# Sample cross-attention: which operand stands and which streams, and one column group per head

## The chip, the cores and the metric

The kernel runs on one core of one Trainium2 chip. The metric is the device time in microseconds; before the change it is the median of three runs.

## The reference, cut to what matters

One layer of a hybrid decoder, for a prompt of 1024 tokens and for a sample group of 8 sequences with 4 tokens each, both with the same weights, d_model 1024, all in fp32. After the mixer comes a cross-attention, 4 heads of 256 dimensions over 256 memory tokens:

```python
def cross_attend(xn, mk, mv, w_xq, w_xo):
    B, L = xn.shape[:2]
    q = (xn @ w_xq).reshape(B, L, N_X_HEADS, X_HEAD_DIM)
    s = jnp.einsum('bqhd,bkhd->bhqk', q, mk.astype(q.dtype)).astype(F32) * (X_HEAD_DIM ** -0.5)
    p = jax.nn.softmax(s, axis=-1).astype(q.dtype)
    o = jnp.einsum('bhqk,bkhd->bqhd', p, mv.astype(q.dtype))
    return o.reshape(B, L, X_WIDTH) @ w_xo
```

For the sample group, keys and values (mk, mv) come from a cache, a separate 1 MB of each for every sequence (8 + 8 MB). An MLP of width 4096 follows.

## The kernel before, in words

Activations stand feature-major in SBUF: hT, and the operand pairs xhi/xlo and yhi/ylo (fp32 split into a high and a low part), each 8 blocks of 128 features by 1056 tokens (1024 of the prompt, 32 of the samples). A weight matrix streams in as "units" of 128 output features: SP loads a unit into raw, ACT makes whi (`split_hi`), DVE makes wlo (`split_lo`, L342), each double-buffered, and TensorE's `product` (L353 to L355) multiplies the unit by a chunk of 352 tokens in 3 x 8 matmuls. There are three chunks. DVE takes the result from PSUM.

The change is in the stage after the prompt's cross-attention. The order of work is written out by hand on every engine, as a list with semaphore waits. On TensorE:

- **Keys**, for each sequence b of 8: `sx_turn(b)` transposes 256 x 1024 keys in 16 transposes (L1035, tile kx; the prompt's probabilities, tile xp, are turned by the same line) into four PSUM banks; then one `xo_product` (unit U_XO + b/2, chunk b%2) runs while ACT and DVE (L1789) evacuate the turned keys to kxT; then `sx_scores(b)` (L1362) multiplies: 16 matmuls whose stationary is a 128x128 block of keys and whose moving operand is 4 query columns.
- **Softmax**: the scores stand keys-major, so DVE copies them to sxT (L1796), TensorE turns them (tile sxT), DVE takes maxima (L1798), ACT the exponential, DVE scales. TensorE meanwhile does both chunks of U_XO + 4, turns the probabilities (tile sxp), and ACT copies them to pxT.
- **Values**, for each of four pairs of sequences: `sx_values` (L1374) twice, each 16 matmuls with a 128x128 block of values as stationary and 4 probability columns moving; then, but for the last pair, both chunks of the next unit.
- **Tail**: ACT and DVE (L1814) make yhi and ylo of the 32 sample tokens from PSUM, and TensorE goes on with w_xo a second time (units U_XB to U_XB + 7), now for chunk 2, which holds the sample tokens.

GpSimd issues the loads of keys (two slots of 1 MB, refilled as soon as the keys of two sequences before are turned) and of the values of sequences 0 to 3; ACT issues those of 4 to 7 (into slots freed by the values of 0 to 3). Ahead of that GpSimd stages the prompt's queries (L676, paced by the prompt's score matmuls of L1311) and copies the sample queries to xqs (L685), since the key slots lie on top of xq. Between the loads it sums squares for the next norm (`xo_squares`). SP's weight loads wait for the split of two units before.

DVE's order in this stage, per unit: evacuate the keys of sequence 2i, add the product to hT (L1781), the same for 2i + 1, then the split of the next unit. An fp32 matmul (not fp32r) leaves two MATMUL and two LDWEIGHTS records, a transpose one of each. Elsewhere in the kernel some lines write into column groups, among them L1117 (window attention; 128 rows, one group of 64 columns, repeated), L1182 (retention state of the prompt, 128 rows, two groups of 64 columns in turn) and L1294 (retention state of the samples, 32 rows, the same two groups in turn).

## Time and profile before

| | before |
|---|---|
| median of three runs | 1763.68 us |
| lowest, highest | 1756.89, 1764.25 us |
| span of the profiled execution, first to last instruction | 1753.1 us |
| TensorE matmuls, busy | 1646.7 us, 94% of the span |
| VectorE, ScalarE, GpSimd busy | 648.0, 443.8, 251.8 us |
| mean granted TensorE clock | 0.946 of full speed |
| read from and written to HBM | 101.19 and 14.16 MB |

The profiled execution is shown by its span; no separate device time of that one execution is given, and the median stands 10.6 us above the span. Times in rows are microseconds from the first instruction. TensorE's busy time is split into PE (matmuls) and PEld (weight loads), which overlap. Busy TensorE is not TensorE at its peak: how many columns stream per weight load, and the granted clock, do not show in that share.

### The profile page before, as it was taken

The page shows a single profiled execution, that of the slowest core. Times are in us where ns is not written, and L with a number is a line of the kernel's source. Part 1 is how long each engine was busy: PE and PEld are TensorE (multiplying, and loading weights), DVE is VectorE, ACT ScalarE, POOL GpSimd, SP SyncE. Part 2 cuts the span into 40 slices and gives each one's busy share as a digit, 9 for nine tenths or more (in the row PEclk, how much of TensorE's full clock was granted, in tenths as well). Part 3 has the DMA queues.
Part 4 walks back from the last instruction along what each step waited for, and adds up shares of the span by engine and source line. Part 5 has one row for each costly group of instructions (what it writes and reads, how often), then busy time and mean ns, then how long its engine had stood idle before and what let it go on. Part 6 is the DMA issues. An engine that isn't in the chain of part 4 may idle for free.

```text
span 1753.1 us, 25903 instructions
## 1 busy us (share of the span) xinstructions
PE 1646.7 (94%) x10206; PEld 1583.2 (90%) x10206; DVE 648.0 (37%) x1170; ACT 443.8 (25%) x779; POOL 251.8 (14%) x310
## 2 busy tenths in 40 slices
PE   5879999988789999789999999999999999999998
PEld 5869777778679999679999999999999999999998
DVE  3532455535544432342221653223322333233322
ACT  4530233323311111241100433003310231023212
POOL 2100100032227500111131400000000000000053
PEclk9989899999869999898887999999999999999999
DMA  5741000010322121022332311111111111111112
GB/s 181 204 182 48 13 25 24 13 45 25 95 96 84 37 95 36 13 97 85 120 109 72 96 49 48 49 48 49 37 48 48 49 48 49 44 40 48 48 36 99
DMA packets 152617, 115.37 MB, mean 66 GB/s; under 512 B 12880, under 2 KB 141968, under 8 KB 152272
## 3 DMA queue, kind: packets, MB, share of 16 engines
q1 hardware_dynamic: 140816, 72.49, 14.2%
q0 software_dynamic: 10576, 37.66, 6.1%
q10 hardware_dynamic: 1152, 4.19, 0.7%
q8 instruction: 51, 0.84, 0.2%
q14 instruction: 22, 0.18, 0.0%
HBM read 101.19 MB, written 14.16 MB: 66 GB/s over the span
## 4 chain that ended last, share of the span: by engine, by line
PE 80%; issue 11%; DVE 5%; ACT 2%; POOL 1%; DMA 1%; ACTq 0%; DVEq 0%; SPq 0%; POOLq 0%
PE ps L353 21%; PE ps L354 20%; PE ps L355 20%; PE ps L1035 5%; PE ps L1374 2%; PE ps L1100 2%; PE ps L1311 2%; PE ps L1329 2%; PE ps L1117 2%; PE ps L1362 2%; DVE wlo L342 1%; DVE xlo L1456 1%; ACT whi L326 1%; PE ps L1175 0%; PE ps L1177 0%
## 5 line engine op out<-in xcount | busy, mean ns | idle before, releaser
L353 PE MATMUL ps<-xhi,whi 128*128 128x352 f32 x1392 | 458.6, 329 | 15.9 <-DVE wlo L342 9.0
L354 PE MATMUL ps<-xlo,whi 128*128 128x352 f32 x1392 | 450.7, 324 | 0.0
L355 PE MATMUL ps<-xhi,wlo 128*128 128x352 f32 x1392 | 450.5, 324 | 0.0
L353 PE MATMUL ps<-yhi,whi 128*128 128x352 f32 x1152 | 381.5, 331 | 3.8 <-DVE xq L1476 1.9
L354 PE MATMUL ps<-ylo,whi 128*128 128x352 f32 x1152 | 376.7, 327 | 0.0
L355 PE MATMUL ps<-yhi,wlo 128*128 128x352 f32 x1152 | 375.6, 326 | 0.0
L353 PEld LDWEIGHTS ps<-xhi,whi 128*128 128x128 f32 x1392 | 265.2, 191 | 28.1 <-issue 17.3
L354 PEld LDWEIGHTS ps<-xlo,whi 128*128 128x128 f32 x1392 | 265.8, 191 | 0.1
L355 PEld LDWEIGHTS ps<-xhi,wlo 128*128 128x128 f32 x1392 | 264.7, 190 | 0.0
L326 ACT ACTIVATE whi<-raw 128x1024 fp32r<-128x1024 f32 x126 | 132.9, 1054 | 437.8 <-PE ps L355 403.1
L353 PEld LDWEIGHTS ps<-yhi,whi 128*128 128x128 f32 x1152 | 223.1, 194 | 4.6 <-issue 2.2
L354 PEld LDWEIGHTS ps<-ylo,whi 128*128 128x128 f32 x1152 | 222.9, 193 | 0.1
L355 PEld LDWEIGHTS ps<-yhi,wlo 128*128 128x128 f32 x1152 | 222.1, 193 | 0.0
L342 DVE TENSOR_TENSOR wlo<-raw,whi 128x1024 fp32r<-128x1024 f32 x130 | 167.9, 1291 | 82.2 <-ACT whi L326 72.7
L1481 DVE TENSOR_TENSOR hT<-ps,hT 128x352 f32 (+1 forms) x120 | 62.7, 523 | 280.2 <-PE ps L355 280.2
L1850 DVE SCALAR_TENSOR_TENSOR relu<-ps,rstd 128x352 f32<-128x352 f32 x96 | 50.3, 524 | 180.4 <-PE ps L355 179.2
L979 ACT ACTIVATE hsq<-relu 128x352 f32<-128x352 f32 x96 | 47.9, 499 | 233.2 <-DVE relu L1850 233.2
L524 POOL TENSOR_TENSOR ss<-hT 128x528 f32<-128x528 f32 (+1 forms) x7 | 6.5, 947 | 669.3 <-DVE hT L1481 655.6
L527 POOL TENSOR_TENSOR sq<-hT 128x528 f32<-128x528 f32 (+1 forms) x50 | 62.9, 1257 | 132.0 <-issue 89.7
L529 POOL TENSOR_TENSOR ss<-ss,sq 128x528 f32<-128x528 f32 (+1 forms) x50 | 66.9, 1337 | 3.9
L1842 DVE TENSOR_TENSOR ylo<-hsq,yhi 128x352 f32 (+1 forms) x96 | 50.5, 526 | 31.2 <-DVE relu L1850 15.8
L716 ACT ACTIVATE yhi<-hsq 128x352 f32 (+1 forms) x96 | 47.8, 498 | 9.8
(271 smaller groups left out, 1548.3 us busy)
## 6 DMA issues: line engine op xcount, KB each, us to landing
raw<-in_w_up SPq DMA_DIRECT2D x32, 512.0 KB
raw<-in_w_down SPq DMA_DIRECT2D x32, 512.0 KB
raw<-in_w_xo SPq DMA_DIRECT2D x16, 512.0 KB
kx<-in_cache_mem_k POOLq DMA_DIRECT2D x16, 512.0 KB, 4.4
raw<-in_w_in SPq DMA_DIRECT2D x14, 512.0 KB, 3.9
spill<-hT POOLq DMA_DIRECT2D x8, 528.0 KB, 6.2
hT<-spill POOLq DMA_DIRECT2D x8, 528.0 KB, 5.0
raw<-in_w_xk SPq DMA_DIRECT2D x8, 512.0 KB
```

Source lines behind the costliest of these rows:

```text
L326: act.activation(whi[:, q], raw[:, q], ACT.Copy).then_inc(s_whi, 1)
L342: dve.tensor_tensor(wlo[:, q], raw[:, q], whi[:, q].bitcast(F32), ALU.subtract).then_inc(s_wlo, 1)
L353: pe.matmul(out, whi[:, q, k, :], x1, start=k == 0, stop=False)
L354: pe.matmul(out, whi[:, q, k, :], x2, start=False, stop=False)
L355: mm = pe.matmul(out, wlo[:, q, k, :], x1, start=False, stop=k == KB - 1)
L527: st.did(pool.tensor_tensor(sq[:, 0:b - a], h, h, ALU.mult))
L529: last = pool.tensor_tensor(ss[:, a:b], ss[:, a:b], sq[:, 0:b - a], ALU.add)
L979: act.activation(hsq[:, b, :], relu[:, b, :], ACT.Square).then_inc(s_sqr, 1)
L1035: return pe.transpose(out, in_, ident[0:n, 0:n])
L1481: return dve.tensor_tensor(chunk(hT, u - m0, c), ps[:, (q + c) % 2, 0:CW], chunk(hT, u - m0, c), ALU.add)
L1842: dve.tensor_tensor(chunk(ylo, u - u0 + q, c), hsq[:, (q + c) % 2, :], chunk(yhi, u - u0 + q, c).bitcast(F32), ALU.subtract).then_inc(s_hl ...
L1850: dve.scalar_tensor_tensor(relu[:, (q + c) % 2, :], ps[:, gemm_bank(u + q, q, c) if q == 0 else (q + c) % 2, 0:CW], 0.0, rstd[:, c * CW:(c ...
```

## The change

Keys and values become moving operands. Queries are kept as qm: for each of the 8 feature blocks and each sequence b a stationary of 32 columns, one per sample token, which is zero but for the 4 columns of b; a score matmul streams 256 keys past it and adds into 32 partitions (one column group per head) of PSUM bank 6, over all sequences. Scores so stand token-major (head, token by key). The copy sxT and its turn go. Probabilities are turned and scattered by ACT into pm, masked in the same way; values stream 256 columns (a head) into a column group per head of bank 2. That output is token-major, so it is copied (osb) and turned (two transposes) ahead of yhi and ylo. GpSimd sets qm and pm to zero. Turned keys are double-buffered by sequence (kT). The second chunk of U_XO + 4 moves behind the turn of the probabilities, and the second chunk of U_XO + 7 behind the last values.

```diff
-        kxT, _ = place("kxT", [P, 2, KB, P], at=at_xl + 24576)
-        sxT, _ = place("sxT", [P, 2, P], at=at_xl)
-        sxp, _ = place("sxp", [P, NM], at=at_xl + 1024)
-        pxT, _ = place("pxT", [P, 2, P], at=at_xl + 2048)
-        xqs, _ = place("xqs", [P, KB, TS], at=at_xl + 32768)
+        kT, _ = place("kT", [P, 2, KB, NM], at=at_xl)
+        qm, _ = place("qm", [P, KB * NB * TS], at=at_xl + 16384)
+        pm, _ = place("pm", [P, 2 * XH * NB * TS], at=at_xl + 24576)
         at_t = at_tab + 4 * 2 * P
+        sxp, _ = place("sxp", [P, NM], at=at_t)
+        osb, _ = place("osb", [P, NM], at=at_t + 4 * NM)
...
+        def own_columns(t):
+            return bass.AP(t, 0, [[t.shape[1], P], [NB * TS, t.shape[1] // (NB * TS)], [TS + DT, NB], [1, DT]])
@@ gpsimd @@
-            pool.tensor_copy(xqs[:], xq[:, :, TP:T]).then_inc(S("sx_q_kept"), 1)
+            pool.wait_ge(s_xs, NQ)
+            pool.memset(qm[:], 0.0).then_inc(S("sx_zeroed"), 1)
+            pool.wait_ge(S("sx_zeroed"), 1)
+            pool.tensor_copy(own_columns(qm), xq[:, :, TP:T].rearrange("p k (b t) -> p k b t", t=DT)).then_inc(S("sx_q_kept"), 1)
...
                 sx_load(pool, b, "cache_mem_v", values_at(b), lambda slot: s_kl[slot])
+            pool.wait_ge(s_xo, NQ)
+            pool.memset(pm[:], 0.0).then_inc(S("sx_zeroed"), 1)
             for m in range(2, KB):
                 xo_squares(m)
@@ scalar @@
-                        wait(act, s_ksc, t - 1)
-                        copy(kxT[:, kb, 0:4, :].rearrange("p k t -> p (k t)"), ps[:, 2 + 2 * kb, :]).then_inc(s_kea, 1)
+                        wait(act, s_ksc, 2 * i + r - 1)
+                        copy(kT[:, r, 0:4, kb * P:(kb + 1) * P], ps[:, 2 + 2 * kb, :].rearrange("p (k t) -> p k t", k=4)).then_inc(s_kea, 1)
...
-            act.activation(sxp[:], ps[:, 7, 0:NM], ACT.Exp, scale=1.0 / 16, bias=wneg[:, 0:1], accum_out=wsum[:, 0:1]).then_inc(S("sx_exp"), 1)
+            act.activation(sxp[:], ps[:, 6, 0:NM], ACT.Exp, scale=1.0 / 16, bias=wneg[:, 0:1], accum_out=wsum[:, 0:1]).then_inc(S("sx_exp"), 1)
             act.wait_ge(S("sx_p_turned"), 1)
-            copy(pxT[:].rearrange("p a r -> p (a r)"), ps[:, 6, 0:2 * P]).then_inc(S("sx_pT_ready"), 1)
+            act.wait_ge(S("sx_zeroed"), 2)
+            copy(own_columns(pm), ps[:, 7, 0:2 * P].rearrange("p (r b t) -> p r b t", b=NB, t=DT)).then_inc(S("sx_pT_ready"), 1)
...
             act.wait_ge(s_vx, NB)
-            copy(yhi[:, :, TP:T], ps[:, 2, 0:KB * TS].rearrange("p (k t) -> p k t", k=KB)).then_inc(s_xoh, 1)
+            copy(osb[:], ps[:, 2, 0:NM]).then_inc(S("sx_o_kept"), 1)
+            act.wait_ge(S("sx_o_turned"), 1)
+            copy(yhi[:, :, TP:T].rearrange("p (h d) t -> p d h t", d=2), ps[:, 3, 0:NM].rearrange("p (d h t) -> p d h t", d=2, h=XH)).then_inc(s_xoh, 1)
@@ tensor, sx_scores(b) @@
-                for kb in range(2):
-                    pe.wait_ge(s_kea, 2 * b + kb + 1)
-                    pe.wait_ge(s_ked, 2 * b + kb + 1)
+                pe.wait_ge(s_kea, 2 * b + 2)
+                pe.wait_ge(s_ked, 2 * b + 2)
+                for dd in range(2):
                     for h in range(XH):
-                        o = kb * P + b * 16 + h * DT
-                        for dd in range(2):
-                            mm = pe.matmul(ps[:, 6, o:o + DT], kxT[:, kb, 2 * h + dd, :], xqs[:, 2 * h + dd, b * DT:(b + 1) * DT], start=dd == 0, stop=dd == 1)
-                    mm.then_inc(s_ksc, 1)
+                        k = 2 * h + dd
+                        mm = pe.matmul(ps[h * TS:(h + 1) * TS, 6, 0:NM], qm[:, (k * NB + b) * TS:(k * NB + b + 1) * TS], kT[:, b % 2, k, :],
+                                       start=b == 0 and dd == 0, stop=b == NB - 1 and dd == 1)
+                mm.then_inc(s_ksc, 1)
@@ tensor, sx_values(b) @@
-                for k in range(KB):
-                    for kb in range(2):
-                        mm = pe.matmul(ps[:, 2, k * TS + b * DT:k * TS + (b + 1) * DT], kx[:, values_at(b) + kb, k * P:(k + 1) * P],
-                                       pxT[:, kb, b * 16 + (k // 2) * DT:b * 16 + (k // 2 + 1) * DT], start=kb == 0, stop=kb == 1)
+                for kb in range(2):
+                    for h in range(XH):
+                        r = (kb * XH + h) * NB + b
+                        mm = pe.matmul(ps[h * TS:(h + 1) * TS, 2, 0:NM], pm[:, r * TS:(r + 1) * TS], kx[:, values_at(b) + kb, h * NM:(h + 1) * NM],
+                                       start=b == 0 and kb == 0, stop=b == NB - 1 and kb == 1)
                 mm.then_inc(s_vx, 1)
@@ tensor, after the eight sequences of keys @@
-            pe.wait_ge(S("sx_s_ready"), 1)
-            for kb in range(2):
-                mm = turn(ps[:, 7, kb * P:(kb + 1) * P], sxT[:, kb, :])
-            mm.then_inc(S("sx_s_turned"), 1)
             pe.wait_ge(s_wlo, U_XO + 5)
             xo_product(U_XO + 4, 0)
-            xo_product(U_XO + 4, 1)
             pe.wait_ge(S("sx_probs"), 1)
             for kb in range(2):
-                mm = turn(ps[:, 6, kb * P:(kb + 1) * P], sxp[:, kb * P:(kb + 1) * P])
+                mm = turn(ps[:, 7, kb * P:(kb + 1) * P], sxp[:, kb * P:(kb + 1) * P])
             mm.then_inc(S("sx_p_turned"), 1)
+            xo_product(U_XO + 4, 1)
             pe.wait_ge(S("sx_pT_ready"), 1)
             for i in range(NB // 2):
+                u = U_XO + 5 + min(i, 2)
                 sx_values(2 * i)
                 sx_values(2 * i + 1)
-                if i < NB // 2 - 1:
-                    u = U_XO + 5 + i
+                if i < 3:
                     pe.wait_ge(s_wlo, u + 1)
                     xo_product(u, 0)
+                if i < 2 or i == 3:
                     xo_product(u, 1)
+            pe.wait_ge(S("sx_o_kept"), 1)
+            for dd in range(2):
+                mm = turn(ps[:, 3, dd * P:(dd + 1) * P], osb[:, dd * P:(dd + 1) * P])
+            mm.then_inc(S("sx_o_turned"), 1)
@@ vector @@
-                        wait(dve, s_ksc, t - 1)
-                        dve.tensor_copy(kxT[:, kb, 4:8, :].rearrange("p k t -> p (k t)"), ps[:, 3 + 2 * kb, :]).then_inc(s_ked, 1)
+                        wait(dve, s_ksc, 2 * i + r - 1)
+                        dve.tensor_copy(kT[:, r, 4:8, kb * P:(kb + 1) * P], ps[:, 3 + 2 * kb, :].rearrange("p (k t) -> p k t", k=4)).then_inc(s_ked, 1)
...
-            dve.wait_ge(s_ksc, 2 * NB)
-            dve.tensor_copy(sxT[:].rearrange("p a r -> p (a r)"), ps[:, 6, 0:2 * P]).then_inc(S("sx_s_ready"), 1)
-            dve.wait_ge(S("sx_s_turned"), 1)
-            st.did(dve.tensor_reduce(wmax[:, 0:1], ps[:, 7, 0:NM], AX.X, ALU.max))
+            dve.wait_ge(s_ksc, NB)
+            st.did(dve.tensor_reduce(wmax[:, 0:1], ps[:, 6, 0:NM], AX.X, ALU.max))
...
-            dve.tensor_tensor(ylo[:, :, TP:T], ps[:, 2, 0:KB * TS].rearrange("p (k t) -> p k t", k=KB), yhi[:, :, TP:T].bitcast(F32), ALU.subtract).then_inc(s_xol, 1)
+            dve.tensor_tensor(ylo[:, :, TP:T].rearrange("p (h d) t -> p d h t", d=2), ps[:, 3, 0:NM].rearrange("p (d h t) -> p d h t", d=2, h=XH),
+                              yhi[:, :, TP:T].bitcast(F32).rearrange("p (h d) t -> p d h t", d=2), ALU.subtract).then_inc(s_xol, 1)
```

## Rows read from the trace of the kernel before

**Rows 1.** The page: busy shares, and the chain that ended last by line.

```profile
PE 1646.7 (94%) x10206; PEld 1583.2 (90%) x10206; DVE 648.0 (37%) x1170; ACT 443.8 (25%) x779; POOL 251.8 (14%) x310
...
PE ps L353 21%; PE ps L354 20%; PE ps L355 20%; PE ps L1035 5%; PE ps L1374 2%; PE ps L1100 2%; PE ps L1311 2%; PE ps L1329 2%; PE ps L1117 2%; PE ps L1362 2%; DVE wlo L342 1%; DVE xlo L1456 1%; ACT whi L326 1%; PE ps L1175 0%; PE ps L1177 
```

**Rows 2.** Stretches (from:to, length; PE, PEld, DVE, ACT, POOL busy (x); clock, DMA share, GB/s).

```profile
794.05:883.31 89.26, 89.26 (x576) 89.26 (x576) 20.23 (x28) 13.36 (x20) 19.04 (x28) 0.81 0.33 112
883.31:895.64 12.33, 11.34 (x54) 11.00 (x55) 2.57 (x7) 1.00 (x4) 3.93 (x6) 0.73 0.15 44
895.64:962.60 66.96, 66.03 (x401) 65.94 (x401) 8.86 (x11) 4.98 (x6) 14.64 (x14) 0.76 0.30 95
962.60:969.30 6.70, 6.70 (x25) 6.70 (x26) 1.23 (x1) 0.41 (x1) 0.00 (x0) 0.56 0.28 78
```

**Rows 3.** Sums of eight stretches each: key turns; then w_xo products; then score matmuls.

```profile
sum 24.48, PE 24.48; mean PE 3.06
...
sum 35.59, PE 35.59; mean PE 4.45
...
sum 29.19, PE 29.19; mean PE 3.65
```

**Rows 4.** The value stretch, with busy time of L1374 alone (PE, PEld).

```profile
895.64:961.60 65.96, 36.79 (x256) 36.94 (x256) 0.77 0.30 96
```

**Rows 5.** Clock: scores, turns, product; state matmuls of L1294; one product at full clock.

```profile
801.30:804.63 3.33, 3.33 (x32) 3.33 (x31) 0.52 (x1) 0.00 (x0) 0.00 (x0) 1.00 0.20 80
804.63:808.04 3.41, 3.41 (x18) 3.41 (x18) 0.69 (x1) 0.60 (x1) 0.00 (x0) 0.50 0.02 5
808.04:811.40 3.36, 3.36 (x23) 3.36 (x22) 0.69 (x1) 1.55 (x2) 1.05 (x2) 1.00 0.40 102
513.30:516.70 3.40, 3.40 (x63) 3.40 (x64) 0.74 (x2) 2.64 (x7) 0.45 (x1) 1.00 0.02 5
...
911.51:915.32 3.81, 3.81 (x25) 1.00 0.00 0
```

**Rows 6.** Timeline of TensorE (start, length, line, tile, shape, records); for L1311 also min/median/max ns.

```profile
769.88 1.04 PE L1035 MATMUL ps<-tab,xp 128*128 128x128 f32 x8
...
775.71 3.62 PE L1311 MATMUL ps<-mkT,stx 128*128 128x256 f32 x16
...
L1311 PE MATMUL ps<-mkT,stx x128: 379/379/767, 708.3 to 779.0; 128*128 128x256 f32 x128
...
201.61 1.93 PE L1117 MATMUL ps<-pT,vtok 128*64 128x512 f32 x4
...
374.85 0.66 PE L1182 MATMUL ps<-vrt,krz 128*64 128x128 f32 x8
375.44 0.44 PE L1035 MATMUL ps<-tab,rk 128*128 128x128 f32 x2
...
374.85 0.42 PEld L1182 LDWEIGHTS ps<-vrt,krz 128*64 128x64 f32 x8
...
513.29 3.71 PE L1294 MATMUL ps<-vrs,kzm 32*64 32x128 f32 x64
```

**Rows 7.** Timeline of GpSimd ahead of the stage; a DMA issue row (median landing).

```profile
760.95 1.04 POOL L676 COPY stx<-xq 128x1024 f32 x1 [8.25 <-PE ps L1311]
...
762.63 2.12 POOL L440 DMA_DIRECT2D kx<-in_cache_mem_k  x4 [0.30 <-POOL xqs L685]
...
kx<-in_cache_mem_k POOLq DMA_DIRECT2D x12, 512.0 KB, 4.3
```

**Rows 8.** Timelines of VectorE and ScalarE around the softmax and at the end.

```profile
880.46 1.66 DVE L342 TENSOR_TENSOR wlo<-raw,whi 128x1024 fp32r<-128x1024 f32 x1
...
884.87 0.42 DVE L1798 TENSOR_REDUCE small<-ps 128x1 f32<-128x256 f32 x1 [0.78 <-PE ps L1035]
...
886.31 0.35 DVE L1556 TENSOR_SCALAR sxp<-sxp,small 128x256 f32<-128x256 f32 x1
...
962.10 0.43 DVE L1814 TENSOR_TENSOR ylo<-ps,yhi 128x256 fp32r<-128x256 f32 x1 [7.37 <-ACT yhi L716]
```

## The prediction

> **What bounds the kernel now.** The page first: TensorE is busy for 94% of the span, and the chain of waits is TensorE lines nearly from end to end; two of them, L1374 and L1362 with 2% each, are the lines that the change rewrites [rows 1]. A microsecond taken out of TensorE's own queue there is a microsecond of the span, unless another engine or a transfer is late next. Then the busy time by stretch, from the first turn of the sample keys (794.05 us) to the end of the first U_XB product (969.30): 89.26 + 12.33 + 66.96 + 6.70 = 175.25 us [rows 2]. TensorE works through nearly all of it, at a mean clock of only 0.56 to 0.81; DVE, ACT and POOL are each busy for a third of it at most, and so are the DMA engines.
>
> The key stage has eight rounds: turns 3.06 us, product 4.45, score matmuls 3.65 on average [rows 3]. In the value stage, L1374 takes 36.79 us, 9.2 per pair of sequences [rows 4]; with 1.0 us of tail (961.60 to 962.60), the six products between share 66.96 - 36.79 - 1.0 = 29.2, or 4.9 each. Both lines load a 128-column stationary to stream four columns past it: 256 records in 29.19 us are 0.114 us each, the spacing of the loads, not of the columns.
>
> The clock is the second thing to see. A stretch of scores alone runs at 1.00; the next, which but for its first 0.3 us holds only turns, at 0.50 (1.2 GHz of 2.4); the next at 1.00 again [rows 5]. So the four-column matmuls are what the clock falls after, and the turns, though slow then, are followed by a rise. In this kernel 64 records in 32*64 tiles, over 3.4 us, ran wholly at 1.00 [rows 5].
>
> **What a new matmul costs.** A score matmul now streams 256 key columns past 32 stationary columns, and its output goes to a quarter of the partitions; four heads in turn use four column groups. Per sequence that is 8 matmuls, or 16 records, in place of 32; the same for values. A record of 256 fp32 columns costs (3.62 - 0.38)/15 = 0.216 us in a row of L1311 [rows 6], 0.38 being a single one's length; one of 128 columns half that, 0.108, with a length of 0.38 - 0.108 = 0.27. *Upper bound:* no overlap between groups, 16 * 0.216 = 3.45 us, what the old scores cost. That records of one column group do not overlap is seen at L1117, which repeats one group: four records of 512 columns in 1.93, 0.48 each where 0.43 would be their columns. *Lower bound:* four at a time, 4 * 0.216 = 0.86. Between them stand L1182 and L1294, which alternate two groups: L1182 has 8 records of 128 columns in 0.66 us, where one after another they would last 8 * 0.108 + 0.16 of tail = 1.02; L1294 has 64 in 3.71, (3.71 - 0.27)/63 = 0.055 each [rows 6]. Groups do overlap, with all 128 rows in use too. The rate that I need for four groups, 0.216/4 = 0.054 per record, is the one at which L1294 was issued, so the queue is no obstacle. I take four at a time. Changing tile shape costs something: from L1182's start to the next line's is 0.59 us, against four slots of 0.108; 0.15 for going in and out [rows 6]. I take 0.24: a score group is 1.1 us, a pair of value groups 8 * 0.216 + 0.22 = 1.95.
>
> The Trainium skill speaks against this (TensorE: Matmul & The Clock Gate, "Packing small matmuls — row/col tiling"): weight loads overlap running matmuls only where the row group differs, and here all four groups share their rows. The trace disagrees: L1182's 8 loads are over in 0.42 us while its matmuls run to 0.66 [rows 6]. Were the page right, an estimate from its columns/1.2 GHz is 27 ns a load, 256 loads, 6.8 us more than my sum.
>
> **The stages, one by one.** *Keys.* Turns: eight full-clock transposes take 1.04 us, (1.04 - 0.27)/7 = 0.11 each [rows 6], so 16 are 1.8 us, if the clock no longer falls. A product alone at 1.00 is 3.81 [rows 5]; 3.9 after another shape. A round is 1.8 + 3.9 + 1.1 = 6.8, eight are 54.4. The idle wait ahead of the first turn stays, and with it that turn's slow clock: 3.06 for 1.8, and some 0.2 on its product, +1.5. Total 55.9 against 89.3.
>
> Cover in that stage: per round DVE is busy for 20.23/8 = 2.5 us and ACT for 1.7 [rows 2], which fits into 6.8. The evacuations' destination is now strided, which I price at nothing. They waited for the previous round's scores, now for those two rounds back: no new wait. K loads: 1 MB is issued when a turn ends and needed two rounds later, 13.6 - 1.8 = 11.8 us; a half lands in 4.3 us, two in about 6 [rows 7]. 112 GB/s at a DMA share of 0.33 over 89.3 us [rows 2] become 112 * 89.3/55.9 = 179 GB/s at a share of 0.53: it fits, though this cover is the thinnest.
>
> *GpSimd ahead of it.* The query copy becomes: wait for the last cross scores, done at 775.71 + 3.62 = 779.3 rather than one block earlier; memset of 2048 columns; copy; then the loads queued behind. A 1024-column copy is 1.04 [rows 7], so the memset is 1 to 3 us, copy 0.4 to 1, four K issues 2.12 [rows 7], landing 4.3 to 6: K data at 779.3 + 3 + 1 + 1.1 + 6 = 790.4 at worst, for turns at 794.05. Cost 0. If that cover were gone, each late microsecond is one. The second memset (after the V issues, ahead of the squares) has over 5 us until ACT needs it: 0; the squares have slack.
>
> *Softmax.* Removed: copy sxT, its turn, and that wait. Added: TensorE reaches the product of U_XO+4 earlier than its weights. DVE's split there lasts 1.66 and starts at 880.46, 0.6 to 0.8 after the product's end (the scores, 3.5 to 3.65 us long, end at 883.31) [rows 8]; so it is done at +2.3 us, scores at +1.1: a new wait of 1.2. Then 3.9; the chain from maximum to probabilities, 884.87 to 886.66, fits inside [rows 8]. Turn 0.25, second product 3.85 (covers ACT's scatter into pm). Total 9.2 against 12.33.
>
> *Values.* 4 * 1.95 = 7.8; 6 * 3.87 = 23.2; the split of each next unit, done 2.3 after a product, is late for values of 1.95: 3 waits of 0.35, 1.0. Total 32.0 against 65.96. V loads have 10 us per pair or more.
>
> *Tail.* The last addition to hT and U_XB's split now follow the last product: ylo is done at 0.6 + 1.66 + 0.43 = 2.7 [rows 8]; two turns and ACT's copies run beside. 2.7 against 1.0, 962.60 less 961.60 [rows 2, 4]. The first U_XB product, 6.70 at clock 0.56 [rows 2], becomes 3.9.
>
> *Sum:* 55.9 + 9.2 + 32.0 + 2.7 + 3.9 = 103.7 against 175.25: 71.5 us less. The span 1753.1 becomes 1681.6. The execution profiled has 10.6 us around its span if it equals the median of 1763.68 (runs reach from 1756.89 to 1764.25): **1692 us**. What a measurement can tell from no change is about 0.5%, 9 us.
>
> **Rivals.** *B, two at a time.* An fp32 matmul is two records in one group; if dispatch holds at the second, only neighbours overlap. Nothing shows four at once; L1294 cannot tell. Then 0.108 per record instead of 0.054: 256 * 0.054 = +13.8, less 2 of waits that vanish: 1704. *C, the clock keeps falling.* Turns stay at 3.06 (+8.8 over seven rounds) and products at 4.45 (+4): 1705; if values bring it down too, six products at 4.9 (+6) and U_XB's 6.70 (+2.8): 1714. For it: short waits are new. Against it: rows 5. The Trainium skill (TensorE: Matmul & The Clock Gate, "PE-mode transpose") says that the full rate does not engage for transposes; here a stretch of hardly anything but turns was followed by 1.00 [rows 5]. By that rule: 1705. *D, the groups do not overlap,* so that the change doesn't do what its placing says: 256 * 0.216 = 55 us; stages 55.9 + 8 * 2.6, 8.0, 28.5 + 23.2, 2.7, 3.9 = 143: 1731. Against it: L1182. *E, slower.* No overlap and the half clock: a 32-column tile counts for little, so the clock falls, and a record costs 0.43. 256 * 0.43 = 110 against the 66 that scores and values take now [rows 3, 4], the rest as before less 3 for the turn gone: +41, 1805. It decides from 69/256 = 0.27 us a record.
>
> **How the numbers follow.** Forecast 0.60 (own range 1682 to 1700), B 0.12, C 0.12, D 0.09, E 0.03, and 0.04 for a late load or memset, half of it costing all the gain. The range 1682 to 1716 takes in the forecast, B and C. Faster 0.95, same 0.02, slower 0.03.
>
> **What would show it.** Right: 16 score records within 1.1 to 1.3 us, starts in fours; turns of 1.8; clock 1.00 from 800 us to the end; a wait of 1.2 for wlo ahead of U_XO+4. B: groups near 2.0. C: digits under 9 in the clock row of the page where turns follow. D: groups of 3.5. The sum is wrong if turns wait on a DMA landing, or if the last key loads start after 785 us.

## The result, and the profile after

The kernel after the change takes 1683.48 us (median of four, 1683.02 to 1685.04) against 1763.23 for the kernel before (four, 1756.89 to 1764.25): a ratio of 0.958, 95% interval 0.955 to 0.961. The forecast was 1692, the range 1682 to 1716.

Its page (busy shares; granted clock in forty slices):

```profile
span 1681.9 us, 25382 instructions
...
PE 1573.4 (94%) x9950; PEld 1498.7 (89%) x9950; DVE 646.8 (38%) x1169; ACT 444.4 (26%) x780; POOL 259.1 (15%) x312
...
PEclk9979899999969999999999999999999999999999
...
PE ps L353 21%; PE ps L354 21%; PE ps L355 21%; PE ps L1047 4%; PE ps L1112 2%; PE ps L1323 2%; PE ps L1341 2%; PE ps L1129 2%; DMA raw<-in_w_xv 1%; DVE wlo L342 1%; DVE xlo L1470 1%; ACT whi L326 1%; DMA raw<-in_w_xk 1%; PE ps L1187 0%; PE
```

The clock row of the page before:

```profile
PEclk9989899999869999898887999999999999999999
```

TensorE's share is 94%, as in [rows 1], so it says nothing of what changed. The two lines with 2% each have left the chain, and 256 of its 10206 matmul records are gone. The digits 8 8 8 7 of the slices where keys and values were are 9 now; the 6 that stands further left in both rows is in the mixer (482 to 526 us before, where TensorE is busy for 37.3 of 43.8 us at a mean clock of 0.67), which the change does not touch.

The stretches after, in the order of [rows 2]: keys, softmax, values, tail, first U_XB product, and all five together.

```profile
794.50:850.05 55.55, 55.55 (x448) 49.12 (x448) 19.04 (x28) 13.36 (x20) 16.86 (x25) 0.97 0.55 183
850.05:859.40 9.35, 8.17 (x55) 7.87 (x51) 2.81 (x6) 1.90 (x4) 7.78 (x9) 1.00 0.21 58
859.40:890.67 31.27, 31.27 (x275) 26.82 (x274) 6.56 (x10) 3.56 (x4) 13.04 (x12) 1.00 0.54 186
890.67:892.70 2.03, 0.17 (x3) 0.00 (x1) 2.03 (x4) 1.33 (x2) 1.45 (x1) 1.00 0.00 0
892.70:898.30 5.60, 5.60 (x25) 5.60 (x26) 1.32 (x1) 0.00 (x0) 2.04 (x2) 0.70 0.64 186
794.50:898.30 103.80, 100.76 (x797) 89.41 (x798) 31.76 (x46) 20.15 (x30) 41.16 (x47) 0.97 0.51 169
```

Keys 55.55, softmax 9.35, values 31.27, tail 2.03, U_XB product 5.60, together 103.80, where [rows 2] sum to 175.25. In the clock column, keys, softmax and values have 0.97 to 1.00 in place of 0.73 to 0.81; the U_XB product has 0.70. TensorE's timeline in the first two rounds, which answers to [rows 3] and [rows 6] (start, length, line, tile, shape, records):

```profile
794.50 3.34 PE L1047 MATMUL ps<-tab,kx 128*128 128x128 f32 x16 [2.63 <-issue]
...
801.86 1.07 PE L1373 MATMUL ps<-kT,qm 128*32 128x256 f32 x16
802.86 1.97 PE L1047 MATMUL ps<-tab,kx 128*128 128x128 f32 x16
804.58 0.41 PE L353 MATMUL ps<-yhi,whi 128*128 128x352 f32 x1
...
808.57 1.07 PE L1373 MATMUL ps<-kT,qm 128*32 128x256 f32 x16
...
859.40 1.93 PE L1387 MATMUL ps<-kx,pm 128*32 128x256 f32 x32
...
890.46 0.38 PE L1047 MATMUL ps<-tab,osb 128*128 128x128 f32 x2
892.70 0.43 PE L353 MATMUL ps<-yhi,whi 128*128 128x352 f32 x1 [1.86 <-DVE ylo L1826]
```

A score group is 1.07 us and a pair of value groups 1.93. Read one by one, the records start in fours, 7 ns apart, and one four follows another after 0.215 us, the spacing at which records of 256 columns follow each other elsewhere (0.216 in the row of L1311 [rows 6]): all four groups stream at the same time. The turn at 802.86 runs at full clock, 1.72 us to the product's first record; the one at 794.50, behind 2.63 us of idle, is still slow. A round is 808.57 - 801.86 = 6.71 us.

TensorE's waits in the same stretch (total, times, longest):

```profile
PE ps L1047 <- issue: 2.6, 1, 2.6
PE ps L353 <- DVE ylo L1826: 1.9, 1, 1.9
PE ps L353 <- DVE wlo L342: 1.2, 1, 1.2
```

The first was there before. The third is the new wait of 1.2 that the prediction had named, the second the tail's. From the first turn to the first MLP matmul the stage took 203.64 us before and takes 132.55 now, 71.1 less; the span fell by 71.2, from 1753.1 to 1681.9. Outside the stage next to nothing moved: the first turn starts at 794.50 for 794.05, and what follows the stage lasts 754.9 us for 755.4. The whole stage before, as a window:

```profile
794.05:997.69 203.64, 200.25 (x1220) 199.57 (x1221) 57.44 (x69) 35.26 (x44) 56.11 (x59) 0.81 0.32 102
```

Cut into stretches of 2 us, that mean clock is 78.5 us at half clock (a granted clock of 0.50). The stage after has 6.8 us of it, behind the idle at 794.50 and behind the tail.

### The profile page after: what moved, and what is told of

Same layout as the page of the kernel before. It is cut to its first block, busy times and chain, and to the rows that moved or that the text cites. A ratio compares the mean times of both kernels' runs of the same rounds, so it can differ in the third digit from the quotient of the medians.

```text
span 1681.9 us, 25382 instructions
## 1 busy us (share of the span) xinstructions
PE 1573.4 (94%) x9950; PEld 1498.7 (89%) x9950; DVE 646.8 (38%) x1169; ACT 444.4 (26%) x780; POOL 259.1 (15%) x312
## 4 chain that ended last, share of the span: by engine, by line
PE 78%; issue 11%; DVE 5%; DMA 2%; ACT 2%; POOL 1%; DVEq 0%; SPq 0%; ACTq 0%; POOLq 0%
PE ps L353 21%; PE ps L354 21%; PE ps L355 21%; PE ps L1047 4%; PE ps L1112 2%; PE ps L1323 2%; PE ps L1341 2%; PE ps L1129 2%; DMA raw<-in_w_xv 1%; DVE wlo L342 1%; DVE xlo L1470 1%; ACT whi L326 1%; DMA raw<-in_w_xk 1%; PE ps L1187 0%; PE ps L1189 0%
## 5 line engine op out<-in xcount | busy, mean ns | idle before, releaser
L353 PE MATMUL ps<-yhi,whi 128*128 128x352 f32 x1152 | 375.0, 326 | 6.0 <-DVE xq L1490 1.9
L354 PE MATMUL ps<-ylo,whi 128*128 128x352 f32 x1152 | 370.9, 322 | 0.0
L355 PE MATMUL ps<-yhi,wlo 128*128 128x352 f32 x1152 | 370.6, 322 | 0.0
L353 PEld LDWEIGHTS ps<-yhi,whi 128*128 128x128 f32 x1152 | 217.4, 189 | 9.0 <-DVE wlo L342 2.9
L354 PEld LDWEIGHTS ps<-ylo,whi 128*128 128x128 f32 x1152 | 217.9, 189 | 0.1
L355 PEld LDWEIGHTS ps<-yhi,wlo 128*128 128x128 f32 x1152 | 217.2, 189 | 0.0
```

Of the source, the lines that this page charges most:

```text
L353: pe.matmul(out, whi[:, q, k, :], x1, start=k == 0, stop=False)
L354: pe.matmul(out, whi[:, q, k, :], x2, start=False, stop=False)
L355: mm = pe.matmul(out, wlo[:, q, k, :], x1, start=False, stop=k == KB - 1)
```

## The experiments

Two theories stood at first. *The overlap*: streams in four column groups run together, the order of issue matters, and the clock stays up because nothing is bound by weight loads any more. *The rivals*: each group has a queue of its own, so order is nothing; or the overlap is small change and the gain is the clock, which four-column matmuls had let fall. "Stage" below is from the first key turn to the first MLP matmul.

### Heads outer

```diff
-                for dd in range(2):
-                    for h in range(XH):
+                for h in range(XH):
+                    for dd in range(2):
```

and the same in sx_values, so that a group gets four records in a row before the next one gets any.

> The changed kernel with only the order of the matmuls altered: all records of one head's column group follow each other (4 in a row) before the next group's. Theory 1 (groups overlap because neighbours in the queue address different groups, and dispatch stays near program order): a group of 16 records lasts about twice as long, 1.9 us instead of 1.07, 16 times, +12 to +14 us on 1683.5, so 1695 to 1698. Rival (each group has a queue deep enough that order doesn't matter): unchanged, 1683 to 1685. Rival (four in a row don't overlap with the next group at all): 3.5 us per group, +36, 1720.

1683.89 us (1678.05 to 1684.99), ratio 0.957 (0.955 to 0.960). TensorE's timeline:

```profile
803.19 1.09 PE L1373 MATMUL ps<-kT,qm 128*32 128x256 f32 x16
804.21 1.97 PE L1047 MATMUL ps<-tab,kx 128*128 128x128 f32 x16
809.92 1.09 PE L1373 MATMUL ps<-kT,qm 128*32 128x256 f32 x16
```

1.09 against 1.07, and the starts still come in fours, now 13 ns apart. The order of issue is not what makes the overlap: records to a busy group did not hold back those behind them for free ones, with four in a row to one group; longer rows were not tried. The prediction's rival B (two at a time) had already lost its price by the 1.07; with this run it loses its reason too, that a record for a busy group holds up those behind it.

### One column group for all heads

```diff
-                        mm = pe.matmul(ps[h * TS:(h + 1) * TS, 6, 0:NM], qm[...], kT[:, b % 2, k, :],
-                                       start=b == 0 and dd == 0, stop=b == NB - 1 and dd == 1)
+                        mm = pe.matmul(ps[0:TS, 6, 0:NM], qm[...], kT[:, b % 2, k, :],
+                                       start=b == 0 and dd == 0 and h == 0, stop=b == NB - 1 and dd == 1 and h == XH - 1)
```

and likewise in sx_values. Same records, same columns, one placement.

> The changed kernel with all heads' scores and values written into one and the same column group (partitions 0 to 31), so the sample cross-attention sums over heads and computes something else; the number, shape and operands of the matmuls stay. Theory 1 (the overlap of four groups is worth 0.162 us a record): 256 records at 0.216 instead of 0.054, +41.5, less 2 to 3 us of waits for the weight split that vanish under them: 1721 to 1723, clock at 1.00 throughout. Rival (swapping the operands alone does it, overlap is not needed): 1683 to 1690. Rival (a 32-column tile by itself counts for little and the clock falls): above 1740, with stretches at 0.50.

1721.14 us (1720.25 to 1723.07), ratio 0.980 (0.977 to 0.982); the stage is 169.76 against 132.55. A score group, and the whole stage's window:

```profile
802.02 3.64 PE L1373 MATMUL ps<-kT,qm 128*32 128x256 f32 x16
```

```profile
798.00:964.00 166.00, 163.61 (x948) 130.94 (x947) 55.42 (x67) 34.88 (x43) 60.42 (x60) 1.00 0.38 124
```

Without overlap, 16 records are 15 * 0.216 + 0.38 = 3.62 by the prediction's prices. So the placement is worth 37 us, and at a clock of 1.00: the other 34 of the 71 have another source.

### Turns twice

```diff
-                    for k in range(KB):
+                    for k in list(range(KB)) * 2:
                         mm = turn(ps[:, 2 + 2 * kb + k // 4, ...], kx[:, slot, k * P:(k + 1) * P])
```

> The changed kernel with every turn of the sample keys issued twice (same input, same output). Theory 1 (turns keep the clock up; it was the four-column matmuls that brought it down): 8 * 16 * 0.108 = +13.8 us, 1697 to 1698, clock 1.00 in the key stage but for the window after the wait ahead of it. Rival (turns do not hold the clock, the short ones in the changed kernel only escape because the rest is dense): clock 0.50 in each round, turns 0.21 each and products slower, +30 or more, above 1713.

1697.6 us (1693.18 to 1699.41), ratio 0.966 (0.964 to 0.968), 13.7 above the change on the same chip (1683.89 with the heads outer). The stretch of seven rounds, and one turn in it:

```profile
798.00:868.00 70.00, 68.82 (x573) 62.31 (x572) 20.48 (x31) 14.06 (x22) 23.55 (x31) 1.00 0.43 144
```

```profile
807.99 3.71 PE L1047 MATMUL ps<-tab,kx 128*128 128x128 f32 x32
```

32 transposes in a row last 3.71 us at full clock, 0.11 each, and the clock stays at 1.00 through the seven rounds. The first turn ran at full clock too (3.69 for 32), behind 2.63 us of idle. Transposes are not what the clock fell after. The Trainium skill (TensorE: Matmul & The Clock Gate, "PE-mode transpose") says that full rate does not engage for them; for fp32 transposes between products this run shows otherwise.

### The kernel before, with 128 columns instead of 4

```diff
-                            mm = pe.matmul(ps[:, 6, o:o + DT], kxT[:, kb, 2 * h + dd, :], xqs[:, 2 * h + dd, b * DT:(b + 1) * DT], ...)
+                            mm = pe.matmul(ps[:, 6, kb * P:(kb + 1) * P], kxT[:, kb, 2 * h + dd, :], xqs[:, 4 * dd:4 * dd + 4, :].rearrange("p k t -> p (k t)"), ...)
...
-                        mm = pe.matmul(ps[:, 2, k * TS + b * DT:k * TS + (b + 1) * DT], kx[...], pxT[:, kb, ...], ...)
+                        mm = pe.matmul(ps[:, 2, (k % 4) * P:(k % 4 + 1) * P], kx[...], pxT[:, kb, :], ...)
```

The old order of work, the old operands and the old number of matmuls; only, each streams 128 columns, those of other tokens and heads among them.

> The kernel before, with the sample score and value matmuls streaming 128 columns instead of 4 past the same stationaries (other query or probability columns beside the right ones, so the sample cross-attention computes something else). Theory 1 (spacing of these records was set by the weight loads, and what brought the clock down was that so few columns streamed): records keep 0.108 to 0.114 us, clock 1.00 in the stage, turns 1.97 and products 3.9: 30 us less than before, about 1733 against 1763. Rival (the clock falls for another reason, as the turns): 1760 to 1765. Rival (128 columns cost more than their loads): above 1765.

1721.8 us (1719.6 to 1724.04), ratio 0.980 (0.978 to 0.982): **more columns, 35 us less** (30 were foretold). TensorE's timeline, and the stage's window:

```profile
810.16 3.73 PE L1362 MATMUL ps<-xqs,kxT 128*128 128x128 f32 x32
813.73 1.91 PE L1035 MATMUL ps<-tab,kx 128*128 128x128 f32 x16
815.40 0.41 PE L353 MATMUL ps<-yhi,whi 128*128 128x352 f32 x1
...
878.08 7.41 PE L1374 MATMUL ps<-pxT,kx 128*128 128x128 f32 x64 [0.47 <-ACT pxT L716]
```

```profile
793.75:963.16 169.41, 165.87 (x1220) 164.97 (x1221) 57.57 (x69) 35.25 (x44) 56.13 (x59) 0.99 0.38 122
```

From its start to the next line's, a score group takes 3.57 us, where [rows 3] has 3.65 on average: 32 records, 0.11 each, with 128 columns as with 4. The turns take 1.67 to the product's first record instead of 3.06, and value pairs 7.41 instead of 9.20. With 3.4 us of half clock left instead of 78.5, the stage is 169.4 against 203.6. TensorE is busy for 98% of it in both, with 1220 records in both; what differs is how many columns stream. Only 4 and 128 were tried, so where between them the clock stops falling is not known.

This kernel and the one-group kernel end at the same time, 1721.8 and 1721.1. Turning the operands round was by itself worth what the clock was worth; it also makes stationaries of 32 columns, which the column groups need, and these brought the rest.

### The same for the scores alone

```diff
-                            mm = pe.matmul(ps[:, 6, o:o + DT], ..., xqs[:, 2 * h + dd, b * DT:(b + 1) * DT], ...)
+                            mm = pe.matmul(ps[:, 6, kb * P:(kb + 1) * P], ..., xqs[:, 4 * dd:4 * dd + 4, :].rearrange("p k t -> p (k t)"), ...)
```

The values keep four columns.

> The kernel before with 128 columns streamed in the score matmuls alone; the value matmuls keep their four columns. Theory 1 (each stage's clock follows from its own matmuls): a round of keys takes 9.16 us as with both changed (11.1 before), the value stage stays at 66 to 67 us with stretches at 0.50: half of the 34 us that both together saved, 15 to 17 us below the kernel before, by stages. Rival (the value stage was slow for another reason and the clock of the key stage decides): 30 or more below.

1743.29 us (1742.43 to 1745.63), ratio 0.993 (0.991 to 0.995), some 12 us less, where 15 to 17 were foretold; the stage is 190.47. Key rounds after the first (799.56 to 871.30), then values (880.59 to 951.90):

```profile
799.56:871.30 71.74, 71.74 (x561) 71.55 (x559) 19.75 (x27) 12.76 (x19) 19.05 (x28) 1.00 0.42 140
880.59:951.90 71.31, 71.31 (x398) 71.31 (x399) 8.43 (x10) 4.06 (x4) 14.63 (x14) 0.70 0.27 89
```

The repaired stage runs at 1.00, the untouched one at 0.70, and it takes 71.31 instead of 65.96 [rows 4]: value pairs of 9.47, 11.64, 9.20 and 11.47 us, where before they were 9.2 on average. The clock follows the matmuls of its own stage. That the value stage got longer, its matmuls untouched, was not expected. By 6 us, in fact, since the window ends 0.6 before the last value record does; that is what is missing from the foretold gain. Its mean clock is 0.70 for the 0.77 of [rows 4]; why more of it fell to the half clock stays open.

### One group for the scores alone

```diff
-                        mm = pe.matmul(ps[h * TS:(h + 1) * TS, 6, 0:NM], ...)
+                        mm = pe.matmul(ps[0:TS, 6, 0:NM], ...)
```

The values keep their four groups.

> The changed kernel with the score matmuls of all heads in one column group and the values still in four (so the sample scores are sums over heads). Theory 1 (overlap is worth 0.162 us a record wherever it is): 8 * (3.64 - 1.07) = 20.6 us, less the 1.2 us wait for the split of U_XO+4 that vanishes: 19.4 us on the changed kernel, 1703. Rival (the overlap of the values is the larger part): under 15.

1699.96 us (1699.58 to 1700.48), ratio 0.968 (0.966 to 0.970); the stage 149.40, 16.9 above the change instead of 19.4. Eight groups are 8 * (3.64 - 1.07) = 20.6 longer; given back are the wait of 1.2 for wlo, which the longer scores hide, and most likely 1.7 for a stretch of half clock behind the tail that this profile doesn't have, though its idle of 1.9 us there is the same.

### Three waits that are left

The first turn waits 2.5 us on "issue", the U_XO+4 product 1.2 on wlo, U_XB 1.9 on ylo. What a single edit takes away:

*The second chunks unmoved:*

```diff
             xo_product(U_XO + 4, 0)
+            xo_product(U_XO + 4, 1)
...
-            xo_product(U_XO + 4, 1)
...
-                if i < 2 or i == 3:
+                if i < 3:
                     xo_product(u, 1)
```

> The changed kernel with the two moved w_xo products back in their old places (the second chunk of U_XO+4 ahead of the turn of the probabilities, the second chunk of U_XO+7 ahead of the last values). Theory 1 (the gain is all in the matmuls and the clock, the moves only trade one wait for another): an idle 0.5 us for ACT's scatter comes back, and the tail waits for two copies, two turns and ylo, about 1.9 us, in place of the 2.1 us that it waits now: 0 to +1 us on the changed kernel, not to be told from it. Rival (the moves carry part of the gain): +3 us or more.

1681.23 us (1676.3 to 1685.82), ratio 0.958 (0.954 to 0.962), the change's own. Its waits besides the first turn's:

```profile
PE ps L353 <- DVE wlo L342: 2.1, 2, 1.2
PE ps L353 <- DVE ylo L1826: 0.9, 1, 0.9
PE ps L1047 <- ACT osb L725: 0.5, 1, 0.5
PE ps L1387 <- ACT pm L725: 0.5, 1, 0.5
```

4.0 us in five waits against 3.1 in two. The moves traded waits; a gain from them was not measured. The profile, of the fastest of the six runs, shows something else, the first turn:

```profile
788.12 1.94 PE L1047 MATMUL ps<-tab,kx 128*128 128x128 f32 x16 [2.59 <-issue]
```

TensorE idles as long ahead of it as ever, and it runs at full clock. So the slow first turn is not in every execution: of eleven profiles with 2.5 to 2.6 us of idle there, eight have it slow (3.2 to 3.4 us) and three don't (this one, the turns twice, and the memsets below with 1.95). Behind the tail's 1.9 us of idle the clock fell in five profiles and stayed at 1.00 in two (one group, and one group for the scores alone). Ahead of the stage too the executions differ by such stretches: this profile has 92 us at half clock there, the change's 102.

*Early splits:* DVE splits the next unit before the addition of the second chunk, here in the keys, and in the values alike.

```diff
+                    if r == 1:
+                        split_lo(dve, i + U_XO + 1, (i + 1) % 2)
                     xo_evacuate(i + U_XO, r)
-                split_lo(dve, i + U_XO + 1, (i + 1) % 2)
```

> The changed kernel with DVE's split of the next w_xo unit ahead of the addition of the second chunk (in the key stage, the value stage and at the end). The changed kernel's trace shows TensorE idle for 1.18 us ahead of U_XO+4 until DVE's split, and 2.0 us ahead of U_XB until ylo, which stands behind an addition and a split. Theory 1: the first goes (-1.2), the second shrinks by the 0.9 us that the split holds ylo up, the three waits among the values were 0.1 each: -2 to -2.5 us on the changed kernel. Rival (my forecast's 0.35 per wait among the values was right and another 1 us hides there): -3.3. Rival (splitting early only moves DVE's queue, keys or additions come late): 0 or above.

1680.86 us (1676.7 to 1682.18), ratio 0.957 (0.953 to 0.960); the wait for wlo is gone, that for ylo halved to 0.9. The 2 us that this should be worth are less than the runs of one kernel differ by, 5 to 10 us on this chip, so the profile shows them and the times do not.

*Early first turn:*

```diff
-            pe.wait_ge(s_xol, NQ)
...
                 sx_turn(b)
+                if b == 0:
+                    pe.wait_ge(s_xol, NQ)
```

> The changed kernel with TensorE's wait for the prompt's last ylo put behind the first turn of sample keys rather than ahead of it. Theory 1 (the one stretch of half clock that is left at 794.8 follows from the 2.6 us of idle ahead of that turn): the idle goes and the clock stays at 1.00, the first turn takes 1.97 instead of 3.34 us: -4 us. Rival (the clock falls there anyway): -2.6 us. Rival (the keys land late, since GpSimd's memset now precedes their loads): the turn still waits, about 0, and the waiter is a DMA.

1677.01 us (1674.77 to 1682.45), ratio 0.955 (0.951 to 0.959). The 2.6 us were no cost of issuing: the wait for the prompt's last ylo stood ahead of turns that don't read it. TensorE's timeline:

```profile
793.48 1.91 PE L1047 MATMUL ps<-tab,kx 128*128 128x128 f32 x16
796.02 0.43 PE L353 MATMUL ps<-yhi,whi 128*128 128x352 f32 x1 [0.63 <-DVE ylo L1787]
```

The turn works through the wait, and 0.6 of it is left. It runs at full clock, 1.91 against 3.34; whether that comes of the missing idle is not shown, since the products unmoved had the idle and the full clock.

### All three, and the tail covered

The two edits above, and on TensorE (with DVE's ylo ahead of its last addition):

```diff
                 sx_values(2 * i + 1)
-                if i < 3:
+                if i < 2:
                     pe.wait_ge(s_wlo, u + 1)
                     xo_product(u, 0)
-                if i < 2 or i == 3:
                     xo_product(u, 1)
+            pe.wait_ge(s_wlo, U_XO + 8)
+            xo_product(U_XO + 7, 0)
             pe.wait_ge(S("sx_o_kept"), 1)
...
             mm.then_inc(S("sx_o_turned"), 1)
+            xo_product(U_XO + 7, 1)
```

> Early splits and early first turn together, and the tail reordered: all values first, then the first chunk of U_XO+7, the two turns of the output, and the second chunk, under which ACT and DVE make yhi and ylo. Theory 1: -2.3 and -4 as in the two kernels alone, and another 1.1 us of the tail's wait: 7 to 7.5 us less than the changed kernel, about 1676 to 1677 where that has 1684. Rival (the last values are asked for before their loads land, as nothing stands between the third and the fourth pair): 1 to 3 us of that is given back to a DMA wait.

**1671.91 us** (1670.52 to 1675.54), ratio 0.952 (0.949 to 0.956), against 1757.07 on that chip: the fastest version, 9 us below the early splits (all six runs below all six) and 5 below the early turn (two of whose six runs are faster than the slowest here). 7 to 7.5 us below the change were foretold; by the profiles it is 10.8 (spans 1671.1 and 1681.9). Of that, 1.7 is clock that the change's profile loses behind its tail, which the forecast had not counted, and 1.0 lies ahead of the last prompt work's end. Its waits from the last prompt work to 900 us, and the stage's window:

```profile
PE ps L1341 <- DVE ylo L1789: 1.6, 1, 1.6
PE ps L353 <- DVE ylo L1789: 0.6, 1, 0.6
```

```profile
790.69:916.26 125.57, 124.10 (x966) 113.03 (x965) 56.93 (x69) 36.50 (x46) 61.51 (x60) 1.00 0.53 174
```

The 1.6 belongs to the prompt's values and was there before. The clock column says 1.00 for the whole stage. That fits the idle as what the clock fell behind; but the products unmoved had 1.00 for the whole stage too, with the idle in it, so one profile doesn't show it.

### Six memsets more

To see how much cover the GpSimd chain ahead of the key loads has, six more memsets of qm stand before the one that is there.

```diff
             pool.wait_ge(s_xs, NQ)
+            for n in range(6):
+                pool.memset(qm[:], 0.0).then_inc(S("sx_zeroed_more"), 1)
+                pool.wait_ge(S("sx_zeroed_more"), n + 1)
```

> The changed kernel with GpSimd's first memset (of qm, 1.81 us in the changed kernel's trace) made seven times in a row, so that the first key loads are issued 10.9 us later, at 793.3 instead of 782.4. A key load lands 4.5 us after its issue (median), the second half half a microsecond later: keys there at 787.5 in the changed kernel, 7.0 us ahead of the first turn. Theory 1 (the memset is hidden under the prompt's last block, with 7 us to spare): 10.9 - 7.0 = 3.9 us more idle ahead of the first turn, ended by a DMA, 4 to 6 us on the whole with the clock's part. Rival (no cover, the memset is on the path already): +10.9. Rival (loads land earlier than I think, or the values' loads held them up): 0 to 2.

1689.76 us (1689.47 to 1692.14), ratio 0.963 (0.961 to 0.965). That is 6.3 above the change's 1683.48 (measured on another chip), near the 4 to 6 of the first theory, but by luck: it did not come as any theory had it. GpSimd, then DVE:

```profile
779.03 11.19 POOL L691 MEMSET qm<- 128x2048 f32 x6 [17.41 <-PE ps L1326]
790.28 1.83 POOL L693 MEMSET qm<- 128x2048 f32 x1
792.18 0.40 POOL L695 COPY qm<-xq 128x256 f32<-128x256 f32 x1
792.87 2.12 POOL L444 DMA_DIRECT2D kx<-in_cache_mem_k  x4 [0.30 <-POOL qm L695]
```

```profile
782.87 0.18 DVE L1570 RECIPROCAL small<-small 128x4 f32<-128x4 f32 x1 [2.01 <-ACT xp L919]
783.08 7.29 DVE L1573 TENSOR_SCALAR xp<-xp,small 128x256 f32<-128x256 f32 x4
790.29 1.21 DVE L1789 TENSOR_TENSOR ylo<-ps,yhi 128x1024 fp32r<-128x1024 f32 x1
```

The loads are issued at 792.87 and the turn starts at 801.72, with its usual 2.5 us of wait and none on a DMA. The late turn comes from DVE: four scalings of the prompt's probabilities, 1.14 us together in the kernel after, last 7.29, each one to the end of a memset, and TensorE waits 5.6 us for them. The subtraction at 790.29, which reads PSUM, runs at its usual 1.2 beside the last memset. The Trainium skill (SBUF — State Buffer, "SBUF: two separate sides") describes a port pair that DVE and GpSimd share and that one instruction holds exclusively; this row agrees, for a memset against an SBUF-to-SBUF scaling. So the question that the run was made for, from when on late key loads cost time, stays open; it shows only that loads issued 8.9 us before the turn were in time.

## Why the prediction was right

The sign, the forecast case and the sum of the stretches held: 103.7 foretold, 103.80 measured; span 1681.6 and 1681.9. Part of that agreement is luck, by its own steps:

- **What a new matmul costs.** "Four at a time", 1.1 and 1.95, measured 1.07 and 1.93. The reasoning was half right. The rate was taken from L1294, and that it fitted is luck: read one by one, its records start in twos, 6 ns apart, and the next two follow after 0.109 us. So its 0.055 is half of what 128 columns take, in two groups, and only happens to equal a quarter of what 256 columns take. The rows of before showed two groups at a time; four were a guess, and the records of the kernel after show them. Nor does the issue rate matter as argued: with the heads outer the groups ran as parallel as before. The rule of the Trainium skill that was weighed there (TensorE: Matmul & The Clock Gate, "Packing small matmuls — row/col tiling"), that weight loads overlap running matmuls only where the row group differs, does not hold here: on the weight-load timeline all 16 loads of a group are over in 0.59 us while its matmuls run for 1.07.

```profile
801.85 0.59 PEld L1373 LDWEIGHTS ps<-kT,qm 128*32 128x32 f32 x16 [0.22 <-issue]
```

- **Keys**, 55.9 foretold, 55.55 measured. A round is 6.71 for 6.8; turns and the slow first one came as priced (that it was slow in this profile is luck too, see the products unmoved). DMA share 0.55 and 183 GB/s for 0.53 and 179, and no turn waited on a landing.
- **GpSimd ahead**, cost 0: the memset took 1.81 us, inside 1 to 3, the copy 0.40, and the loads were issued at 782.40.

```profile
779.83 1.81 POOL L690 MEMSET qm<- 128x2048 f32 x1 [17.40 <-PE ps L1323]
781.70 0.40 POOL L692 COPY qm<-xq 128x256 f32<-128x256 f32 x1
782.40 2.22 POOL L444 DMA_DIRECT2D kx<-in_cache_mem_k  x4 [0.30 <-POOL qm L692]
```

  The right number for an incomplete reason: the seven memsets show that the danger on this engine was first what it holds up on DVE, and only then its loads.
- **Softmax**, 9.2 and 9.35, with the 1.2 for wlo where it was said to be.
- **Values**, 32.0 and 31.27. "3 waits of 0.35" don't show among TensorE's waits, since the splits there take 1.22 us and not the 1.66 that the row at 880.46 [rows 8] had lent them. (The split ahead of U_XO+4 did take 1.65, beside additions of GpSimd; so the 1.2 of the softmax came out.)

```profile
859.95 1.22 DVE L342 TENSOR_TENSOR wlo<-raw,whi 128x1024 fp32r<-128x1024 f32 x1
```

- **Tail**, 2.7 and 2.03, and **the first U_XB product**, 3.9 and 5.60. The second is a miss: its clock is 0.70, half speed for 3.4 us from 893.8 on, behind the tail's idle. The sum had priced that idle as time waited and not as clock lost after it, though the first turn, in the same sum, had been given exactly that. "Clock 1.00 from 800 us to the end", the prediction's sign, misses this stretch. The 1.7 too many here hide the 0.35, 0.73 and 0.67 too few of keys, values and tail; with these errors of both signs, 103.80 for 103.7 is closer than the terms are.
- **Sum to time.** This is the term that was mis-sized, by 8.7 us: "10.6 us around its span". Every run whose span is on record stands 1.8 or 1.9 above it. The profiled execution of before was thus one of about 1755 us, faster than all four runs shown, whose median stands 8 higher. In all its runs beside the experiments, on three chips, that kernel took from 1747.76 to 1766.11; in its eleven runs on one of them the lowest, of span 1746.0, had a mean clock of 0.950, the highest, 1764.3, one of 0.937. The kernel after's four runs lie within 2 us; but versions near it spread over 5 to 10 us (1678.05 to 1684.99 with the heads outer, 1676.3 to 1685.82 with the products unmoved), so that it varies less is not shown. Against the median the change gained 79.8; on the chip of the first four experiments it gained 73 (1756.77 to 1683.89, with the heads outer), and in the profiles 71.2. The difference in the sum, 71.5, was right; the time that it was taken from was not.

Of the rivals, B fell by the 1.07 and by the heads outer; C by the turns twice and by the clock of 1.00 from 798.2 to 893.8 (the falls that did come have other places, each behind idle); D's price was right (1731 less the 10.6 is a span of 1720.4, and with one group it was 1719.8), but its condition isn't met; E needed both no overlap and the half clock, and without overlap the clock was 1.00.

## What to carry to other kernels

A busy TensorE whose clock digits fall below 9 is worth a try before any restructuring: find the matmuls that stream few columns per weight load, and give them more columns, even useless ones, at the same spacing; here, from 4 to 128 columns, that alone was half of the gain. The other half comes from small stationaries in different column groups; in both orders of the loops that were tried it was the same. Then look for waits that stand ahead of work which doesn't need them: idle TensorE costs its own length and, in most profiles here but not in all, a slow stretch behind it. And look at several executions before a few us are put down to a cause: stretches at half clock come and go between them.

## What the runs showed of the hardware that was not expected

- Matmuls for four column groups, all 128 rows in use, ran four at a time whichever way they were issued: 16 records in 1.07 and 1.09 us against 3.64 in one group, 3.4 times as fast with what changing shape costs.
- The clock fell with TensorE busy all the time: at nearly the same spacing of records (32 in 3.65 and 3.57 us) the stage with 4 columns per load had 78.5 us at half clock, the one with 128 columns 3.4. Why is open.
- Behind 2.5 to 2.6 us of idle ahead of the first turn the clock was at half in eight profiles and at full in three.
- A GpSimd memset (128 x 2048 fp32, 1.81 us) held a DVE scaling from SBUF to SBUF until it ended: four of them, 7.29 us instead of 1.14.
